# Expert 0 in a 64-slot block at the head of the expert blocks, and slots spread over the partitions

## What is computed

```python
logits = (x2 @ w_router + b_router)
top_v, top_i = lax.top_k(logits, 4)
gates = softmax(top_v)
def expert_block(xe, e):
    gu = xe @ w_gate_up[e] + b_gate_up[e]           # 1024 -> 2048
    gate = minimum(gu[:, :1024], 7.0)
    up = clip(gu[:, 1024:], -7.0, 7.0)
    h = gate * sigmoid(1.702 * gate) * (up + 1.0)
    return h @ w_down[e] + b_down[e]                # 1024 -> 1024
y = sum over a token's four experts of gate * expert(x)
```

## Time and profile before

| | us |
|---|---|
| median of 3 runs | 1327.01 (1326.57 to 1328.63) |
| the profiled execution, its own time | 1326.56 |
| its span, first to last instruction | 1324.7 |
| PE busy | 1230.7 (93%) |
| DVE busy | 827.7 (62%) |
| ACT busy | 610.0 (46%) |
| POOL busy | 146.0 (11%) |
| DMA, hardware queue | 80.7% of sixteen engines' span |
| DMA, software queue | 6.8% |

### The profile page before, as it was taken

How to read it: one execution, slowest core, us unless ns; L and a number is a source line. 1 busy time by engine, 2 the same in 40 slices (tenths; PEclk the granted TensorE clock), 3 DMA queues, 4 the chain that set the end, 5 groups by cost and what they waited for, 6 DMA issues and landing times.

```text
span 1324.7 us, 18569 instructions
## 1 busy us (share of the span) xinstructions
PE 1230.7 (93%) x6270; PEld 795.8 (60%) x6273; DVE 827.7 (62%) x1333; ACT 610.0 (46%) x822; POOL 146.0 (11%) x171
## 2 busy tenths in 40 slices
PE   7999999899999999999999999999999999999981
PEld 5888864475747478474747364747477374747720
DVE  3896758693928299283837463928398283749703
ACT  4111242372727367263535352736377264537602
POOL 9100012010000100001010100010100001010011
PEclk9999999979999999999999999999999899999996
DMA  9610178399999999999999998999999999999995
GB/s 320 95 40 1 38 236 334 129 301 402 416 410 419 412 418 407 403 419 414 418 398 419 390 387 316 419 416 419 414 418 394 382 418 383 422 405 422 381 390 190
DMA packets 67295, 457.49 MB, mean 345 GB/s; under 512 B 15758, under 2 KB 19538, under 8 KB 34456
## 3 DMA queue, kind: packets, MB, share of 16 engines
q1 hardware_dynamic: 56344, 435.28, 80.7%
q0 software_dynamic: 10880, 21.30, 6.8%
HBM read 439.99 MB, written 23.24 MB: 350 GB/s over the span
## 4 chain that ended last, share of the span: by engine, by line
PE 41%; DMA 17%; DVE 14%; issue 5%; ACT 2%; DVEq 0%; POOL 0%; SPq 0%; ACTq 0%; POOLq 0%
PE bank L2273 22%; DMA ring_lo<-in_w_gate_up 11%; PE bank L2413 10%; DVE w_lo L2557 10%; DMA ymix<-ffn_in,idx_next 4%; PE bank L2424 3%; DMA w_out<-in_w_down 2%; ACT w_hi L2051 1%; PE bank L2256 1%; PE bank L2263 1%; DVE cmix L2575 1%; PE bank L2363 1%; DVE h_lo L2570 1%; PE bank L2389 1%; DVE cmix L2578 1%
## 5 line engine op out<-in xcount | busy, mean ns | idle before, releaser
L2557 DVE TENSOR_TENSOR w_lo<-ring_lo,w_hi 128x1024 fp32r<-128x1024 f32 x271 | 316.7, 1219 | 91.2 <-ACT w_hi L2051 88.7
L2051 ACT ACTIVATE w_hi<-ring_lo 128x1024 fp32r<-128x1024 f32 x271 | 272.4, 1053 | 79.5 <-DMA ring_lo<-in_w_gate_up 45.9
L2413 PE MATMUL bank<-ring_lo,x_s 128*64 128x512 f32 x832 | 187.3, 597 | 0.0
L2273 PE MATMUL bank<-w_hi,x_hi 128*128 128x512 f32 x544 | 177.1, 407 | 9.5 <-DVE x_lo L2563 7.4
L2273 PE MATMUL bank<-w_lo,x_hi 128*128 128x512 f32 x544 | 171.3, 397 | 0.0
L2273 PE MATMUL bank<-w_hi,x_lo 128*128 128x512 f32 x544 | 170.3, 395 | 0.0
L2557 DVE TENSOR_TENSOR w_lo<-w_out,w_hi 128x1024 fp32r<-128x1024 f32 x136 | 161.6, 1218 | 7.3 <-ACT w_hi L2051 7.3
L2051 ACT ACTIVATE w_hi<-w_out 128x1024 fp32r<-128x1024 f32 x136 | 141.0, 1055 | 32.1 <-PE bank L2273 32.1
L1946 POOL DMA_INDIRECT token_sums<-ymix,row_cur x32 | 53.5, 1670 | 728.6 <-ACT ymix L2081 728.6
L2273 PEld LDWEIGHTS bank<-w_hi,x_hi 128*128 128x128 f32 x544 | 100.4, 193 | 43.9 <-issue 16.6
L2273 PEld LDWEIGHTS bank<-w_lo,x_hi 128*128 128x128 f32 x544 | 104.4, 192 | 22.8
(11 more groups left out here) (474 smaller groups left out, 1442.9 us busy)
## 6 DMA issues: line engine op xcount, KB each, us to landing
ring_lo<-in_w_gate_up SPq DMA_DIRECT2D x128, 2048.0 KB, 18.9
w_out<-in_w_down SPq DMA_DIRECT2D x128, 1024.0 KB, 20.4
ring_lo<-in_w_in SPq DMA_DIRECT2D x3, 2048.0 KB, 21.3
w_out<-in_w_out SPq DMA_DIRECT2D x2, 2048.0 KB, 9.4
x<-in_x_prompt SPq DMA_DIRECT2D x6, 512.0 KB, 11.6
ring_lo<-in_w_in SPq DMA_DIRECT2D x2, 1024.0 KB, 10.2
token_sums<-x SPq DMA_DIRECT2D x4, 512.0 KB
ffn_in<-hf SPq DMA_DIRECT2D x4, 512.0 KB, 5.9
```

The lines of the kernel that those rows point to most:

```text
L2051: nc.scalar.activation(high(j), raw(j), ACT.Copy).then_inc(s["w_hi"], 1)
L2273: last = nc.tensor.matmul(bank[b + u][:], v[:, k, :], part(j)[:, u, :], start=(j == 16 and first), stop=(k == KD - 1 and part is high and ...
L2413: last = nc.tensor.matmul(bank[2 * half][64 * u:64 * u + 64, :], x_s[:, k % 4, 64 * (k // 4):64 * (k // 4) + 64], gu[:, k, :, half, 256 * ...
L2557: v.tensor_tensor(low(j), raw(j), high(j).bitcast(F32), ALU.subtract).then_inc(s["w_lo"], 1)
```

## The change

- Expert 0 is handled in a small block at position 0. The first run of pairs is four long and starts there: small, wide, small, wide, ... The last wide block before the two quarters goes. There are 16 wide, 14 small and 2 quarter blocks. Ranks 1 to 16 are wide as before.
- The router's last part prepares a small block in place of a wide one: a gather of half rows, four transposes, one copy to *x_s*; the first split of weights and of x goes.
- *iota_s*, *iota_h* and *iota_q* are permuted, so that slot numbers in sequence stand in partitions that are apart: in *iota_s* slot s stands in partition 8 (s mod 16) + 4 (s div 16 mod 2) + s div 32, in *iota_h* in 4 (s mod 16) + s div 16 of its half, in *iota_q* in 4 (s mod 8) + s div 8 of its quarter. A plain copy *iota_c* serves the rest of the router.
- The sides (*row_cur*, *gate_cur*) and the loads' waits move by one position with this.

```diff
-PAIRS = (3, 3, 3, 3)
-FIRST_EXTRA = 1 + 2 * PAIRS[0]
+PAIRS = (4, 3, 3, 3)
+FIRST_EXTRA = 2 * PAIRS[0]
-THIRD_EXTRA = SECOND_EXTRA + 1 + 2 * PAIRS[3]
-FINAL = THIRD_EXTRA + 2
+FINAL = SECOND_EXTRA + 2 + 2 * PAIRS[3]
-SMALL_RANK = sum(PAIRS) + 5
+SMALL_RANK = sum(PAIRS) + 4
...
-        g.indirect_dma_start(xg, None, scratch["hf"], ...
+        g.indirect_dma_start(xg[:, 0:D // 2], None, scratch["hf"].rearrange("t (c d) -> (t c) d", c=2), ...
...
-        for h in range(2):
-            act.wait_ge(*((s["gT_psum"], 3), (e["xT_psum"], 1))[h])
-            nc.scalar.activation(tb["x_hi"][:, 4 * h:4 * h + 4, :]..., bank[XT_BANK[h]][:], ACT.Copy)
+        act.wait_ge(e["xT_psum"], 1)
+        nc.scalar.activation(tb["x_s"][:, :, :].rearrange("p j t -> p (j t)"), bank[4][:], ACT.Copy)
...
-            v.tensor_copy(tb["iota_s"][:], iota_i[:])
-            v.tensor_copy(tb["iota_h"][:].rearrange("p (h c) -> p h c", h=2), iota_i[:, 0:S_SLOTS].unsqueeze(1)...)
+            v.tensor_copy(iota_c[:], iota_i[:])
+            v.tensor_copy(tb["iota_s"][:].rearrange("p (e f b) -> p e f b", e=16, f=2), iota_i[:].rearrange("p (b f e) -> p e f b", e=16, f=2))
+            v.tensor_copy(tb["iota_h"][:].rearrange("p (h a b) -> p h a b", h=2, b=4),
+                          iota_i[:, 0:S_SLOTS].rearrange("p (b a) -> p a b", b=4).unsqueeze(1)...)
...
-        v.tensor_scalar(tb["idx_next"][:], sel0[:], MISS, tb["spare"][:, 0:1], ALU.add, ALU.min).then_inc(e["idx"], 1)
+        v.tensor_scalar(row0[:], sel0[:], MISS, tb["spare"][:, 0:1], ALU.add, ALU.min).then_inc(row_in, 1)
+        dve.wait_ge(row_in, row_in0 + 1)
+        v.tensor_scalar(tb["idx_next"][:], row0[:], 2.0, tb["upper"][:, 0:1], ALU.mult, ALU.add).then_inc(e["idx"], 1)
...
-        load_behind_wide(expert_at(sp, 1), 1, 0, True)
...
-        wide(0, 0, expert_at(pe, 1), 2)
...
-        with pe.Fori(0, PAIRS[0] - 1) as i:
+        pair(0, 0)
+        with pe.Fori(1, PAIRS[0] - 1) as i:
             pair(0, i)
...
-        pair(3, PAIRS[3] - 1, 1)
-        wide(THIRD_EXTRA, SMALL_RANK - 1, expert_at(pe, FINAL - 1), 4)
+        pair(3, PAIRS[3] - 1, 4)
```

More of the change, by code:

```diff
@@ L1074, in loop_tables @@
         "idx_next": sb(stack, "idx_next", [P, 1], I32),
[L1075 to L1078, removed]
+        "x_s": sb(stack, "x_s", [P, MT, P]),
     }
@@ L1982, in _ @@
             add_bias(q)
-        gather(1, 2)
+        gather(1)
         for q in range(3, NT):
@@ L1986, in _ @@
         pool.wait_ge(keep["bd_added"], 16 * NT)
-        scatter(0, 0)
+        scatter(0, 0, 2)
+        gather(2, 2)
+        added(0)
+        scatter(1, 1)
         def pair(run, i, side, next_parts=2):
@@ L1996, in pair @@
             scatter(q + 1, 1 - side)
-        with pool.Fori(0, PAIRS[0] - 1) as i:
-            pair(0, i, 1)
-        pair(0, PAIRS[0] - 1, 1, 1)
+        with pool.Fori(1, PAIRS[0] - 1) as i:
+            pair(0, i, 0)
+        pair(0, PAIRS[0] - 1, 0, 1)
         gather(FIRST_EXTRA + 1, 2)
         added(FIRST_EXTRA - 1)
-        scatter(FIRST_EXTRA, 1)
+        scatter(FIRST_EXTRA, 0)
         with pool.Fori(0, PAIRS[1]) as i:
-            pair(1, i, 0)
+            pair(1, i, 1)
         gather(TOP)
@@ L2144, in take_x_rest, with small @@
             nc.scalar.activation(xs_rest[:, :, :].rearrange("p j t -> p (j t)"), bank[5][:, 0:256], ACT.Copy).then_inc(r["x_s"], 1)
-        def small(q, side, sq, loads, lq, with_rest=False):
+        def small(q, side, sq, loads, lq, with_rest=False, first=False):
             for half in range(2):
@@ L2155, in small @@
                 nc.scalar.activation(h_s[:, 2 * half:2 * half + 2, :].rearrange("p j t -> p (j t)"), bank[5][:, c], ACT.Copy).then_inc(s["h_hi"], 1)
[L2156 to L2157 removed]
+            split(loads + 1, lq, 0, first)
+            split(loads + 1, lq, 1, first)
             take_x(q + 1)
[L2159 to L2160 removed]
+            split(loads + 1, lq, 2, first)
+            split(loads + 1, lq, 3, first)
             if with_rest:
@@ L2164, in small @@
             take_y(q, side, [4], [512])
-            split(loads + 1, lq, 4)
-            split(loads + 1, lq, 5)
+            split(loads + 1, lq, 4, first)
+            split(loads + 1, lq, 5, first)
         def quarter_hidden(q, sq, turned):
@@ L2180, in _ @@
         act.sem_inc(s["y_free"], 1)
-        for j in range(1, SLOTS):
-            split(1, 0, j, first=True)
-        wide(0, 0, 0, 2, 1)
         def pair(run, i, side, next_parts=2):
@@ L2690, in _ @@
         v.tensor_reduce(sel[:], bank[6][:, 208:214].rearrange("p (a c) -> p a c", a=2), AX_X, ALU.add).then_inc(t["sel"], 1)
-        for j in range(1, SLOTS):
-            split(0, j)
-        wide(0, 0, 0, expert_at(dve, 1), 2, 0, blocks_back=0)
         def pair(run, i, side, next_parts=2):
```

175 lines of the change are left out of this document (81 added, 94 removed).

## The result

| | before | after |
|---|---|---|
| median | 1326.8 us (1326.4 to 1328.6) | 1309.0 us (1308.4 to 1309.8) |
| ratio | | 0.9864 [0.9847, 0.9881] |
| span of the profiled execution | 1324.7 us | 1308.0 us |
| last load of the second block's expert lands | 318.4 us | 321.4 us |
| last load of all lands | 1300.1 us | 1284.0 us |

What follows compares the result with a forecast made beforehand. The prediction took the DMA engines to pace the blocks. Its terms, 11.0 + 0 + 0.9 + 1 = 12.9 us off the profiled 1326.56, gave 1313.7, forecast as 1314 us (own range 1307 to 1319; 8 in 10: 1304 to 1324).

Steps and rivals of the forecast that it cites:

- term 1: Gathers and scatters of the expert blocks: slots spread over the partitions even the engines' rows, 11.0 us gained.
- The rests as the measure: Expert blocks: DMA idle time, from each stretch's share below 1.01 and its length, 20.6 us, bounds the spreading's gain.
- forecast of 10 to 13 us: Wide blocks with 70 to 80 rows: their gathers would land in 10 to 13 us where they took 15.9.
- rival B: Expert blocks: spreading the slots evens nothing, only the head and the end gain, 1325 us; chance 0.16.
- Term 2: Expert 0 in a small block: TensorE saves 11.9 us, but the kernel gains 0 us, range 0 to 3.
- Term 3: The head: less work starts the first block 1.3 us earlier, less 0.4 for the row index, net 0.9 us.
- The cover: The head: bias additions keep the DMA queues full while the next expert's loads go out late; without it, up to 4 us.
- Term 4: The end: the last wide block follows a small one, so the DMA rests less before the last two experts, 1 us.
- C: The head: DMA engines run dry in the first small block and every later load is 4 us late, 1331 us; chance 0.06.
- D: The expert blocks: TensorE becomes the bound; held impossible in the pairs, given no time of its own.
- A: Expert blocks and end: all the DMA idle time comes back, the end lag too, 1305 us; chance 0.13.

Runs made afterwards that it cites:

- placement only: The changed kernel with its three slot tables back in plain order, so only the new order of blocks is kept: 1325.44 us, ratio 0.9986.
- aligned kernel: The changed kernel with other slot tables, by which wide and small lists crowd the same eight engines: 1329.18 us, ratio 1.0014.
- spread-only kernel: The kernel before the change with the permuted slot tables alone, expert 0 still in a wide block: 1309.51 us, ratio 0.9869.
- filler: The changed kernel with six more TensorE products in each small block, their result unused: 1309.15 us, ratio 0.9871.

## Why the prediction was right, and where it was off

**The bound** was right: a pair needs the DMA engines' time, not TensorE's. 12.8 us of added products cost nothing, while rows taken off the software queue give 31 us. Expert weights came every 32.1 us, forecast 32.0.

**The mechanism of term 1** was right, and its size was the error: 11.0 us forecast, 16.2 measured (placement only against the changed kernel, 1325.4 - 1309.2). Two things in its working failed.

- *The rests as the measure.* By the formula of the prediction the rests left are 2.9 + 3.8 + 5.5 us (784.0, 833.0 and 1258.7 on) and 0.2 in the small block from 568.7 on: 12.4 in place of 20.6, 8.2 given back. But the stretch of the 30 experts is 19.1 us shorter. Of the other 10.9, 3.0 are a shift at the start: the second block's expert is in at 321.4, not 318.4. This is no lost DMA time, since the share there stays at 1.00 or more. And the hardware queue's packets took 81.4% of 1308.0 us in place of 80.7% of 1324.7 (the table ahead of the prediction), 1064.7 against 1069.0: 4.3 less for the same bytes. (The aligned kernel, crowded as before, has 80.6% of 1328.4, 1070.7 again.) What is left, 3.6 us, lies within the rounding of two-digit shares. So the rests are only about half of the cost of a lag, and the packets themselves took longer.
- *"So the gain is from wide ones."* Halving the rows evens the two halves of the partitions, not the engines within a half. The small and quarter tables carry 4.4 of the 16.2 us. And the lists of 65 to 81 rows are nine of sixteen, not ten.

Another sum was at hand that needs no shares: the excess rows, counted by the map that the prediction cites, times the price of a row from the earlier trace rows, (51.8 - 18.2) x 0.49 = 16.5 us.

**The reading of the earlier trace rows** came to a true conclusion by an unsound step. Equal landing times with a third fewer rows were taken as the sign of crowded engines. The changed kernel, from 403 and from 893.7 us on:

```profile
q0 software_dynamic: 288, 0.94, 14.9%
...
ymix<-ffn_in,idx_next POOLq DMA_INDIRECT x1, 14.4
...
q0 software_dynamic: 288, 0.62, 9.9%
...
ymix<-ffn_in,idx_next POOLq DMA_INDIRECT x1, 14.3
```

They are still equal, and only some 1.5 us shorter. The forecast of 10 to 13 us failed; taken alone, the landing times ("if gathers take 15 us as before") would have spoken for rival B, which the spread-only kernel refutes. Two rows fewer on the busiest engine are 2 x 0.49 = 1.0 us, which is about what went. The rest of a landing is not set by the rows: it is the same for 0.94 and for 0.62 MB. It goes with the moment of the issue instead. Before, the gathers of whole rows that were issued while a small block ran took 13.6 to 17.1 us from 376 us on; the one behind the block with the rest rows (809.2), where the DMA share is 0.86, took 11.8, and three issued while a wide block ran (475.2, 969.0, 1196.5) took 11.2 to 11.7. That the difference is the wait behind queued weights is likely, but wasn't tested.

**TensorE's and ScalarE's waits** (in all, times, longest) show where the time does not appear:

```profile
ACT w_hi L2039 <- DMA ring_lo<-in_w_gate_up: 49.2, 27, 3.6
...
PE bank L2242 <- DMA ymix<-ffn_in,idx_next: 4.4, 6, 1.2
```

PE's wait for gathers fell from the 15.0 us of the earlier trace rows to 4.4. The split waits for weights a little more than the 45.9 before, with the pace of the loads faster: TensorE and ScalarE are still ahead of them.

**Term 2**, 0 us for TensorE's 11.9, held: there are 0.3 us between the spread-only kernel and the changed one, and the filler says the same.

**Term 3**, 0.9 us, can't be judged from one pair of traces. The head of the changed kernel, and last the first product in its second measurement:

```profile
269.19 1.09 PE L1512 MATMUL bank<-ident,ymix 128*128 128x128 f32 x4
...
270.32 0.60 ACT L1380 ACTIVATE x_s<-bank 128x512 f32<-128x512 f32 x1 [0.27 <-PE bank L1512]
...
272.22 3.68 PE L2399 MATMUL bank<-ring_lo,x_s 128*64 128x512 f32 x8 [1.37 <-issue]
...
273.07 3.68 PE L2399 MATMUL bank<-ring_lo,x_s 128*64 128x512 f32 x8 [1.45 <-issue]
```

The transposes take 1.09 us in place of 1.95 and x_lo is gone, so from the first transpose to the first product it is 3.03 us in place of 4.62, 1.6 less where 1.3 were forecast. But the transposes begin at 269.19 in place of 267.92. Of these 1.3, 0.7 are there already at VectorE's first copy of a slot table (200.52 against 199.78), before anything that the change touches in the head. So the first block starts 0.3 us earlier in this pair, and 0.5 later in the second measurement. The eleven traces with the new head have it at 272.1 on average, the two with the old one at 272.5 and 274.0: a gain of about 1 us is possible, and the spread is as large. The small block lasts 26.0 us (to 298.2), forecast 27, with the clock at 0.98 from 276 to 290. The cover held: the DMA share from 276 to 290 us is 1.00.

**Term 4**, 1 us for the end, isn't seen apart. With term 3 it makes the placement, 1.9 forecast and 1.7 measured with the plain tables. That agreement is luck as far as the runs show: the excess of rows explains 2.0 us by itself, and the prediction had no term for it; beside the new tables, where its sum puts the 1.9, only 0.3 are left. The last stretch rests as before, 5.5 us by the share of 0.80, so the sum was right to withhold the 3.1 us there.

**The rivals.** B is refuted by the spread-only kernel, C by the DMA share in the head, and D, TensorE as the bound, by the filler. B's own time, 1325, lay outside the range of 1304 to 1324 that was said to take in most of it. A (1305) was too high in its gain for this change, because the rests around the rest rows stayed; better tables reach it, though.

## What to carry to other kernels

Where partial lists of rows are gathered or scattered beside a stream that fills the DMA engines, count the rows of each engine over the lists together, not in one list, and multiply the busiest one's excess by the price of a row. The cure is cheap: a table that spreads the slots, and a different order in lists that alternate, so that the odd row falls to another engine each time. Make the tables in few operations off the path that the start waits for. A mean DMA share below that of full stretches, with loads queued, is the sign; but it understates the loss.

## What the runs showed of the hardware

- An engine's lag isn't gone when the block is over. Two kernels with the same crowding in each list differ by 12.0 us (1317.2 and 1329.2), by whether wide and small lists, which alternate every 24 to 36 us, crowd the same engines.
- Engines that lag take longer for the same bytes of weights, too: by the hardware queue's share 1064.7 us each in the changed kernel, 1069.0 before and 1070.7 in the aligned one.
- A scattered row that adds in HBM takes 0.33 us of an engine for 4 KB, and a row in and out 0.49 together, so the way in is about half as dear as the way out.
- With 23 small copies on VectorE, 3.8 us by the rows above, the first block at the other end of the mixer started at 276.7 us, where eleven traces without them have 270.9 to 273.4.
- Open: with the rows nearly even, the DMA engines still rest at the end and in the stretch with the rest rows (0.80 and 0.85 in the changed kernel), and some 2 us that the rows' count would give don't come.
